# A two-block transformer kernel on one core: lat's weights in two transfers, ada0's column stage joined to ada1's, the memory input loaded and transposed earlier

## The reference

```
# first block
h = rms(x, mix_norm_g); p = h @ w_in            # columns: q, kv, k_rot | hyena (3 x 512)
a = mla(p...)                                   # 8 heads, latents normalised, rope
h = hyena(p..., rfft(filters(hy_w1, b1, freq, w2, b2, w3, b3, decay)))
x = x + concat(rms(a), rms(h)) @ w_out
x = x + mem_xattn(rms(x, cross_norm_g), rms(mem, mem_norm_g))   # K, V of 256 memory tokens
x = x + hier_moe(rms(x))                        # 4 groups x 8 experts, 2 taken per token
# second block
mod = silu(c) @ w_ada + b_ada                   # 6 x 1024 shifts, scales and gates
u = modulate(x, ...); x = ... hybrid_mixer(u)   # RG-LRU and block attention
u = modulate(x, ...); x = ... hierarchical_moe(u)
```

## Time and profile before

| | us |
|---|---|
| median of 3 runs | 1044.98 |
| lowest, highest | 1040.83, 1046.42 |
| the profiled execution | 1044.6 |
| its span (first to last instruction) | 1042.6 |
| PE busy in the span | 996.1 |
| DVE busy | 586.5 |
| ACT busy | 351.5 |
| POOL busy | 20.2 |

### The profile page before, as it was taken

How to read it: one execution, slowest core, us unless ns; L and a number is a source line. 1 busy time by engine, 2 the same in 40 slices (tenths; PEclk the granted TensorE clock), 3 DMA queues, 4 the chain that set the end, 5 groups by cost and what they waited for, 6 DMA issues and landing times.

```text
span 1042.6 us, 15038 instructions
## 1 busy us (share of the span) xinstructions
PE 996.1 (96%) x5360; PEld 606.1 (58%) x5360; DVE 586.5 (56%) x1105; ACT 351.5 (34%) x676; POOL 20.2 (2%) x41
## 2 busy tenths in 40 slices
PE   8999999999999999999999999999989999999985
PEld 7668566977968633434344579876753434434434
DVE  5735427555355646444444585787765655555546
ACT  5653424445444222212222355743531111111113
POOL 1000001000000000000000000000000000000000
PEclk9999999999998999999999999989999999999998
DMA  9255572446408499999999828430709999999931
GB/s 362 114 238 212 210 302 108 162 182 242 162 1 332 167 368 425 426 425 425 424 427 424 356 81 360 171 156 1 282 12 385 424 425 424 428 423 427 423 133 41
DMA packets 28896, 289.06 MB, mean 277 GB/s; under 512 B 3080, under 2 KB 5544, under 8 KB 7728
## 3 DMA queue, kind: packets, MB, share of 16 engines
q1 hardware_dynamic: 25344, 282.04, 66.0%
q0 software_dynamic: 1136, 3.74, 1.2%
q10 hardware_dynamic: 2368, 2.64, 0.8%
HBM read 287.34 MB, written 1.06 MB: 277 GB/s over the span
## 4 chain that ended last, share of the span: by engine, by line
PE 52%; DVE 9%; ACT 3%; issue 2%; DVEq 1%; ACTq 0%
PE bank L977 22%; PE bank L991 11%; PE bank L997 6%; PE bank L984 4%; PE bank L625 1%; DVE ring_r L482 1%; PE bank L627 1%; PE bank L626 1%; PE bank L1097 1%; PE bank L950 1%; PE bank L1098 1%; ACT ring_r L475 1%; PE bank L1086 0%; PE bank L1138 0%; PE bank L1052 0%
## 5 line engine op out<-in xcount | busy, mean ns | idle before, releaser
L977 PE MATMUL bank<-ring,arena 128*64 128x512 f32 x1040 | 237.5, 598 | 1.4 <-DVE arena L2218 1.4
L482 DVE TENSOR_TENSOR ring_r<-ring,ring_r 128x1024 fp32r<-128x1024 f32 (+1 forms) x84 | 99.2, 1212 | 91.3 <-ACT ring_r L475 91.3
L2232 DVE TENSOR_REDUCE arena<-bank 128x512 f32 x130 | 83.7, 686 | 118.7 <-PE bank L997 116.1
L977 PEld LDWEIGHTS bank<-ring,arena 128*64 128x64 f32 x1040 | 69.3, 136 | 123.8 <-issue 123.8
L991 PE MATMUL bank<-ring,arena 128*64 128x512 f32 x520 | 127.4, 611 | 1.8 <-DVE arena L2354 1.5
L475 ACT ACTIVATE ring_r<-ring 128x1024 fp32r<-128x1024 f32 (+1 forms) x84 | 84.8, 1046 | 83.2 <-PE bank L627 82.1
L625 PE MATMUL bank<-HT_r,ring_r 128*128 128x256 f32 x352 | 102.0, 290 | 7.1 <-DVE arena L1899 3.2
L627 PE MATMUL bank<-HT_r,ring_r 128*128 128x256 f32 x352 | 100.3, 285 | 0.0
L1568 ACT ACTIVATE arena<-bank 128x512 f32<-128x512 f32 x64 | 38.3, 598 | 150.9 <-PE bank L977 150.9
L997 PEld LDWEIGHTS bank<-tab,arena 128*128 128x128 f32 x520 | 55.7, 140 | 55.6 <-issue 49.6
L625 PEld LDWEIGHTS bank<-HT_r,ring_r 128*128 128x128 f32 x352 | 68.2, 194 | 10.4 <-issue 8.9
(11 more groups left out here) (429 smaller groups left out, 1422.5 us busy)
## 6 DMA issues: line engine op xcount, KB each, us to landing
ring<-in_experts SPq DMA_DIRECT2D x64, 2048.0 KB, 15.1
ring<-in_experts SPq DMA_DIRECT2D x64, 1024.0 KB, 11.5
ring<-in_ada SPq DMA_DIRECT2D x12, 2048.0 KB, 9.7
ring<-in_win SPq DMA_DIRECT2D x5, 2048.0 KB, 12.7
ring<-in_hy SPq DMA_DIRECT2D x3, 2048.0 KB, 19.1
ring<-in_mk SPq DMA_DIRECT2D x2, 2048.0 KB, 8.7
ring<-in_mv SPq DMA_DIRECT2D x2, 2048.0 KB, 9.6
ring<-in_wo SPq DMA_DIRECT2D x2, 2048.0 KB, 7.5
```

The source lines that it names most:

```text
L482: nc.vector.tensor_tensor(R(w), w, R(h), ALU.subtract).then_inc(sem("w_low"), 1)
L977: last = mm(gu_bank[g:g + WIN, :], xw[:, k, :], w[:, k * 512:(k + 1) * 512], start=k < 2, stop=k >= KD - 2)
L2232: last = V.reduce_sum(ysT[:, 4 * u:4 * u + 4, bass.ds(s, WIN)], dT_bank[u][:, :].rearrange("p (c g w) -> p c w g", c=4, g=2), AXX)
```

## The change

1. The first quarter of lat's weights becomes a transfer of its own with its own semaphore (`lat_in`), issued ahead of the filters' argument inputs (`feat`); the rest of lat is issued behind them. ACT and DVE split chunk 0 of lat before they evacuate hT(0, 1). On DVE the first sine argument is moved behind these evacuations. The filler ahead of lat has 3 pairs in place of 5.
2. ada0 is pinned to bank 6. Its column stage adac0 goes, and ada_col(1) does the columns of ada0 and ada1 together. ada0's slot is vacated with ada1's. All later banks of the rotation change.
3. The memory tokens get a buffer of their own in the arena, free after the first spectrum product. ACT issues their load at the first head, and squares them at the fourth and fifth; DVE normalises them at the sixth. PE transposes them ahead of the second convolution, the filler ahead of mk goes, and DVE takes their low parts before `gated(1)`.
4. Two pairs of semaphores in the router become two semaphores; DVE waits once where it waited twice.
5. The fillers ahead of cnt2 and gx2 have 10 pairs in place of 8. Three matmuls of 256 columns follow gu_T in the extra window.

```diff
-          ("hy1", 2), ("hyT0", 2), ("latT", 2), ("ada0", 1), ("hy2", 2), ("hyT1", 2), ("adac0", 1),
+          ("hy1", 2), ("hyT0", 2), ("latT", 2), ("ada0", 1, (6,)), ("hy2", 2), ("hyT1", 2),
...
-STAGES += [("cv1", 2), ("memT", 4), ("mk", 4), ("mv", 4), ...
+STAGES += [("memT", 4), ("cv1", 2), ("mk", 4), ("mv", 4), ...
...
 LAST.update({f"ada{_i}": (f"adac{_i}", 0) for _i in range(12)})
+LAST["ada0"] = LAST["ada1"]
...
-        junk, junk_m = area(16384, 1024), area(4096, 1024)
+        junk = area(16384, 1024)
+        mem, junk_m = three(area(4096, 2048), TT), hytok[:, :, 0, :]
...
-            arrived(act, name)
+            if (name, chunks) == ("lat", (0,)):
+                act.wait_ge(sem("lat_in"), 16)
+            else:
+                arrived(act, name)
...
+            sp.dma_start(ring[:, slot(1), 0:2 * LAT], A["lat"][:, 0:2 * LAT]).then_inc(sem("lat_in"), 16)
             sp.dma_start(ring[:, slot(0), at:at + FEAT], A["filt"][:, at:at + FEAT]).then_inc(sem("feat"), 16)
-            load(PLACE["lat"], A["lat"], dict(UNITS)["lat"])
+            sp.dma_start(ring[:, slot(1), 2 * LAT:KD * LAT], A["lat"][:, 2 * LAT:KD * LAT]
+                         ).then_inc(sem(f"slot_full{slot(1)}"), 16)
...
             def ada_col(i):
-                ready(pe, f"ada{i}")
+                parts = (0, 1) if i == 1 else (i,)
+                for n in parts:
+                    ready(pe, f"ada{n}")
                 ps = take(pe, f"adac{i}")
-                for c in range(4):
-                    last = mm(ps[:, c:c + 1], ada_sum(i)[:, c * P:(c + 1) * P], ones[:, 0:1], start=True, stop=True)
+                for a, n in enumerate(parts):
+                    for c in range(4):
+                        last = mm(ps[:, 4 * a + c:4 * a + c + 1], ada_sum(n)[:, c * P:(c + 1) * P], ones[:, 0:1],
+                                  start=True, stop=True)
...
-            occupy("lat", 0, 5, still[:, 0:P], still[:, P:P + 256])
+            occupy("lat", 0, 3, still[:, 0:P], still[:, P:P + 256])
...
             hyena_tok(1)
-            ada_col(0)
...
+            transposed("memT", mem, KD, "xn_m")
             convolve(1)
-            transposed("memT", XN, KD, "xn_m")
-            occupy("mk", 0, 5)
-            channel_out("mk", ["mk0", "mk1"], HT, low_m, banks_of("memT"))
+            channel_out("mk", ["mk0", "mk1"], HT, low_x, banks_of("memT"))
...
-                occupy(f"cnt{b}", 0, 8 if b == 2 else 6)
+                occupy(f"cnt{b}", 0, 10 if b == 2 else 6)
...
-                occupy(f"gx{b}", 0, 8 if b == 2 else 6)
+                occupy(f"gx{b}", 0, 10 if b == 2 else 6)
...
                         gu_T().then_inc(sem(f"extra_gT{b}"), 1)
+                        for _ in range(3):
+                            mm(d_bank[0][:, 0:256], ident, T("iota")[:, 0:256], start=True, stop=True)
...
+            high(act, "lat", (0,))
             high_evac("hT", HT, (0, 1), lambda k: C("mix_norm_g", k))
-            high(act, "lat", (0,))
+            high(act, "lat", (1,))
             high_evac("hT", HT, (2, 3), lambda k: C("mix_norm_g", k))
-            high(act, "lat", (1,))
...
-                if h + 2 == H1 - 1:
-                    act.dma_start(XN, A["mem"]...).then_inc(sem("mem_in"), 16)
+                if h == 0:
+                    act.wait_ge(sem("product"), TT)
+                    act.dma_start(mem, A["mem"]...).then_inc(sem("mem_in"), 16)
+                if h in (3, 4):
+                    act.wait_ge(sem("mem_in"), 16)
+                    act.wait_ge(sem("zed"), TT)
+                    square(junk_m, three(mem[:, h - 3, :], 2), ssq_m[:, h - 3:h - 2])
             high(act, "mk0", (0, 1))
-            act.wait_ge(sem("mem_in"), 16)
-            squares("m", lambda t: XN[:, t, :], lambda t: junk_m, ssq_m, lambda t: None)
...
-                act.wait_ge(sem("e_diff"), b)
-                A_(ex2, m2, ACT.Exp).then_inc(sem("e_exp"), 1)
-                act.wait_ge(sem("g_diff"), b)
-                A_(gex, cand4, ACT.Exp).then_inc(sem("g_exp"), 1)
+                act.wait_ge(sem("diffs"), 2 * b - 1)
+                A_(ex2, m2, ACT.Exp).then_inc(sem("exps"), 1)
+                act.wait_ge(sem("diffs"), 2 * b)
+                A_(gex, cand4, ACT.Exp).then_inc(sem("exps"), 1)
...
-            sine_argument("f1", "hy_b1", C("hy_freq", 0, 1, FFN))
+            low(dve, "lat", (0,))
             got(dve, "hT", 3)
             low_evac("hT", HT, low_x, (0, 1), lambda k: C("mix_norm_g", k))
-            low(dve, "lat", (0,))
+            sine_argument("f1", "hy_b1", C("hy_freq", 0, 1, FFN))
+            low(dve, "lat", (1,))
             low_evac("hT", HT, low_x, (2, 3), lambda k: C("mix_norm_g", k))
-            low(dve, "lat", (1, 2, 3))
+            low(dve, "lat", (2, 3))
...
-            modulation(0)
...
                 if h == 5:
+                    normalised("m", lambda t: mem[:, t, :], lambda t: mem[:, t, :], rstd_m, "xn_m")
                     spectrum_product(1)
-            normalised("m", lambda t: XN[:, t, :], lambda t: XN[:, t, :], rstd_m, "xn_m")
             low(dve, "mk0", (0, 1))
+            low_evac("memT", HT, low_x, 4, lambda k: C("mem_norm_g", k))
             gated(1)
             dve.wait_ge(sem("zed"), 2 * TT)
-            low_evac("memT", HT, low_m, 4, lambda k: C("mem_norm_g", k))
...
-                dve.wait_ge(sem("e_exp"), b)
-                dve.wait_ge(sem("g_exp"), b)
+                dve.wait_ge(sem("exps"), 2 * b)
```

More of the change, by code:

```diff
@@ L184 @@
         STAGES += [("zs1", 4)]
-STAGES += [("cv1", 2), ("memT", 4), ("mk", 4), ("mv", 4), ("mixT", 4), ("wo", 4), ("ada7", 1), ("cT", 4), ("adac7", 1), ("mq", 4),
+STAGES += [("memT", 4), ("cv1", 2), ("mk", 4), ("mv", 4), ("mixT", 4), ("wo", 4), ("ada7", 1), ("cT", 4), ("adac7", 1), ("mq", 4),
            ("xs0", 1), ("xs1", 1)]
@@ L853, in _ @@
                     z_spectrum(1)
+            transposed("memT", mem, KD, "xn_m")
             convolve(1)
-            transposed("memT", XN, KD, "xn_m")
-            occupy("mk", 0, 5)
-            channel_out("mk", ["mk0", "mk1"], HT, low_m, banks_of("memT"))
-            token_out("mv", ["mv0", "mv1"], HT, low_m, banks_of("memT"))
+            channel_out("mk", ["mk0", "mk1"], HT, low_x, banks_of("memT"))
+            token_out("mv", ["mv0", "mv1"], HT, low_x, banks_of("memT"))
             for j in range(4):
@@ L1427, in _ @@
                     mla_exp(h + 2)
-                if h + 2 == H1 - 1:
-                    act.dma_start(XN, A["mem"].rearrange("(t p) d -> p t d", p=P)).then_inc(sem("mem_in"), 16)
+                if h == 0:
+                    act.wait_ge(sem("product"), TT)
+                    act.dma_start(mem, A["mem"].rearrange("(t p) d -> p t d", p=P)).then_inc(sem("mem_in"), 16)
+                if h in (3, 4):
+                    act.wait_ge(sem("mem_in"), 16)
+                    act.wait_ge(sem("zed"), TT)
+                    square(junk_m, three(mem[:, h - 3, :], 2), ssq_m[:, h - 3:h - 2])
             high(act, "mk0", (0, 1))
-            act.wait_ge(sem("mem_in"), 16)
-            squares("m", lambda t: XN[:, t, :], lambda t: junk_m, ssq_m, lambda t: None)
             ready(act, "pv7")
@@ L1886, in modulation @@
                 ps = got(dve, f"adac{i}")
-                m = mod[:, 4 * i:4 * i + 4]
-                free(V.tensor_tensor(m, ps[:, 0:4], C("b_ada_2", 4 * i, 4), ALU.add), f"adac{i}")
+                i0 = 0 if i == 1 else i
+                n = 4 * (i + 1 - i0)
+                free(V.tensor_tensor(mod[:, 4 * i0:4 * i0 + n], ps[:, 0:n], C("b_ada_2", 4 * i0, n), ALU.add), f"adac{i}")
             def outer_taps(third):
@@ L2138, in moe @@
                 V.tensor_tensor(M12, M1, M2, ALU.add).then_inc(sem("hot"), 1)
-                V.tensor_tensor(m2, i2, m1, ALU.subtract).then_inc(sem("e_diff"), 1)
+                V.tensor_tensor(m2, i2, m1, ALU.subtract).then_inc(sem("diffs"), 1)
                 V.tensor_tensor(cand4, lgg, gmx.unsqueeze(2).broadcast_to([P, TT, G]), ALU.subtract
-                                ).then_inc(sem("g_diff"), 1)
+                                ).then_inc(sem("diffs"), 1)
                 if b == 1:
```

## The result

The changed kernel takes 1041.75 us (median of 12 runs, 1039.65 to 1044.11) against 1044.51 (12 runs, 1040.83 to 1048.4). The ratio is 0.9974, interval 0.9962 to 0.9986: 2.8 us faster, where 7 were forecast. The time lies in the forecast's range and the direction is right, but the gain is 2.8 of 7.0 us, within the 0.5% that I called no change. The profiled execution took 1040.8, its span 1038.3.

What follows compares the result with a forecast made beforehand. PE, busy for 96% of the span, was taken as the bound. The terms -1.7 - 4.6 + 0 + 4.7 - 3.1 - 0.7 - 1.6 = -7.0 took the median 1044.98 to 1038.0 us, range 1030.5 to 1045.0.

Steps and rivals of the forecast that it cites:

- The start: First lat projection: with its first quarter loaded early, PE starts sooner and the last layer comes earlier; gain 1.7 us.
- Rival (d): Start: the new order changes nothing, since the sine argument takes lat's place; 1039.7 us, chance 0.11.
- hy2's banks: At hy2: banks freed earlier remove 3.0 us of PE's wait and the 1.6 us slow stretch behind; gain 4.6.
- ada0's columns: ada column stages: eight small matmuls move to ada1's stage and cancel those removed; 0 us.
- ada3: Attention stage: late slot release delays ada3's load; 2.95 us stall plus 1.7 slow stretch, a loss of 4.7.
- the signs of being wrong: ada3 landing over 10 us after issue, mk waiting for DVE, or attention-stage clock falling for longer than 4 us.
- My step for the memory's share: ada3's load: the memory input beside it takes bandwidth and delays its landing by 1.3 us, bounds 0 and 2.5.
- The memory part: Memory stage: transposes ahead of the second convolution let mk follow it directly; gain 3.1 us.
- yl: Before the yl projection: the shifted bank rotation removes PE's 0.69 us wait for a copy; gain 0.7 us.
- The extra window: Extra window: three matmuls fill 1.45 us of idle, so the eight following take 1.96 instead of 3.51; gain 1.6.
- The router's fillers: Second router: the longer fillers add 0.9 us, each into a wait such as 1.65 us; 0 us.
- Rival (a): Attention stage and others: ada3's stall eats most of the gain, slow stretches stay; 1044 us, half 1041; chance 0.22.

Runs made afterwards that it cites:

- before; again: The unchanged kernel before, run once more for a second profile: 1042.9 us, one run.
- 1 slot early: The changed kernel with ada0's slot freed after its product: 1037.63 us, ratio 0.9938 to the kernel before.
- 2 own column: The changed kernel with ada0's own column stage on a pinned bank and its slot freed as in the kernel before: 1037.67 us, ratio 0.9932.
- 3 own column, late: The changed kernel with ada0's own column stage, its slot still released with ada1's: 1040.96 us, ratio 0.9977 to the kernel before.
- 4 short fill: The changed kernel with 8 pairs in place of 10 in the second router's two fillers: 1040.67 us, ratio 0.9965 to the kernel before.
- 5 argument first: The changed kernel with ada0's slot freed early and the filters' argument inputs issued ahead of lat's first quarter: 1038.65 us, ratio 0.9933.
- 6 old start: The changed kernel with ada0's slot freed early and the start part undone: 1037.53 us, ratio 0.9938 to the kernel before.
- 7 memory later: The changed kernel, slot still late, with the memory input issued at the third head and its squares one head later: 1039.43 us, ratio 0.9949.
- 8 no cover: The changed kernel with ada0's slot freed early, without the three matmuls in the extra window: 1038.44 us, ratio 0.9930.
- 10 old memory part: The changed kernel with ada0's slot freed early and the memory part as in the kernel before: 1041.3 us, ratio 0.9965.
- 11 banks only: The kernel before with only the bank and column part of the change, ada0's slot freed after its product: 1040.69 us, ratio 0.9956.
- 12 combined: The changed kernel with ada0's slot freed early, the old start and the second router's short fillers: 1038.39 us, ratio 0.9932.

## Why the prediction was wrong

Three quantities from the fourteen profiles, in us, each from the timeline of PE, carry the verdicts (L921 is the router's first line in the kernel before; it is L929 in the changed one):

| kernel | filters' last layer starts | hy2's first matmul to the last V product | second router's L921 to the first expert |
|---|---|---|---|
| before; again | 26.40; 25.24 | 84.33; 84.33 | 27.55; 27.57 |
| changed | 25.41 | 87.47 | 29.58 |
| 1 slot early | 25.39 | 82.97 | 27.53 |
| 2 own column | 27.19 | 82.98 | 27.95 |
| 3 own column, late | 26.53 | 90.11 | 27.50 |
| 4 short fill | 25.77 | 88.71 | 27.50 |
| 5 argument first | 27.93 | 82.98 | 29.64 |
| 6 old start | 26.37 | 82.98 | 29.62 |
| 7 memory later | 26.33 | 85.89 | 29.61 |
| 8 no cover | 26.21 | 82.97 | 27.53 |
| 10 old memory part | 27.00 | 84.62 | 29.60 |
| 11 banks only | 26.24 | 84.63 | 28.75 |
| 12 combined | 26.39 | 84.65 | 27.60 |

**The start (forecast -1.7): wrong, 0.** The eight kernels with the new start (5 set apart) have the last layer at 26.2 in the mean (25.4 to 27.2), the five with the old one at 26.1 (25.2 to 26.4). The step that failed is "filt's argument about 1.0 to 1.4 later". In all eight it lands at 9.6 to 10.0, 2.2 to 2.6 later than the 7.34 of the earlier trace rows. I left out the 0.47 us by which SP issues it later (3.05 for 2.58), and took the landing of a small transfer as its bytes over the rate. So in the changed kernel the argument (L683, now L690) moves by 2.5 us and the transposes behind it by 1.6 (8.76 to 10.37), not by the 0.2 to 0.5 of the forecast. PE then idles for 1.7 to 3.4 us, where it had under 0.6 in four of the five profiles of the old start. In six of the eight a slow stretch begins there and ends before 17 us; three of the five old starts have one too. The second stop, at lat's second chunk, came, 1.65 later than forecast (17.75 for 16.1), and that is what the last layer is late by (25.41 for 23.7). Kernel 11, with the old start, an argument landing at 9.9 and no slow stretch, has its last layer at 26.24, 1.0 later than the second profile of before; so a late argument costs the old start too. Rival (d) had the value right, no gain at the start, but not the reason.

**hy2's banks (-4.6): right.** 3.9 at hy2, less the 1.0 that came from the start in that profile, is 2.9 of wait. The slow stretch behind it went in every profile: 84.33 in the table against 82.97 makes 1.4, together 4.3. Kernel 11 has 4.6 by its ratio for this and yl, where 5.3 were forecast.

**ada0's columns (0): right**, kernels 1 and 2.

**ada3 (+4.7): right in its mechanisms, about right in its size.** The column of the table grows from 82.97 to 87.47, 88.71 and 90.11 with the late slot, by 4.5, 5.7 and 7.1, the last beyond my bound of 5.9, and by 2.9 with the memory input out of the way. The medians give 4.1 (changed less kernel 1) and 3.3 (kernel 3 less 2), the ratios 3.8 and 4.7. In the changed kernel's own profile a slow stretch ahead of ada3 took part of the time that PE would else have waited, so it is in part luck that its 4.5 meets 4.7: I had 2.95 of stall and 1.7 behind it, and it has 1.52 of stall and a slow stretch on either side. The sentence that an idle of 3 us was twice followed by a slow stretch misread its rows: one of the two idles was 2.06 us, and in the second profile of before 2.30 us at the same place had none. Of the signs of being wrong that I had named the changed kernel showed none: 9.1 us for ada3's landing, no wait of mk for DVE, two slow stretches of 3.4 us each. Kernel 3, with the same late slot, showed two: 10.8 us, and a slow stretch of 6.8.

My step for the memory's share (1.3, from the 12.2 us in the earlier trace rows) was too low: 1.7 to 3.4. I had set the Trainium skill's rule ("DMA: Bandwidth & Descriptors", Queues, rings and completion order: turns between queues) aside by that row. Where ACT issues the memory input 0.7 us ahead of the ada load, as in the changed kernel and in kernels 1, 4, 5, 6, 8 and 12, it lands in 4.9 to 5.4 us. 4.9 is 214 GB/s, half of the 426 that the window shows; that fits turns of equal size, and their 2.5 for ada3 is near the 1.7 to 2.2 measured there. But in kernels 2 and 3 it was issued 0.2 us behind the ada load and took 17.4 and 16.8, and in kernel 7, issued behind three of SP's loads that were still under way, 17.7. Equal turns alone don't give that, and why the order weighs so much stays open. The 12.2 of the row lies between: its memory input was issued behind a load that was still under way.

**The memory part (-3.1): right**, 3.6 in the profiles (12.74 to 9.16), and 3.7 between the medians of kernels 10 and 1 (2.8 by their ratios).

**yl (-0.7): right.** Before, 20.5 us after the wait at 638.46 came another of 0.69; it is gone in every profile with the new banks.

**The extra window (-1.6): half of it.** The forecast took one slow stretch for the rule. Without the three matmuls it came in two profiles of four (3.51 and 3.57 us for the eight matmuls, against 1.94 and 1.94), with them in none of ten. The mean gain is 0.8, from four profiles.

**The router's fillers (0): wrong, about +1.** The step "0.9 us, each into a wait such as the 1.65" holds only at full clock. In the nine profiles with long fillers the stage took 27.5 us where the clock held (three), 27.95 with a shorter slow stretch, and 29.6 in all five where it fell for 6 us or more. The two longer fillers can't be left early: at half clock the first ends after its data are there (6.81 us for 20 instructions in place of 16). With short fillers it took 27.5 to 27.6 four times and 28.75 once, with slow stretches in three of the five; the 28.75 is the only one of them with a slow stretch as long as 6.8 us, and 0.85 less than the 29.6. The stage by itself misleads, though, because a slow stretch in it goes with less time just before it (the last section). From L1207 (products at 682 us, ahead of the router) to the first expert all nine with long fillers took 90.5 to 90.9, the five with short ones 88.7, 89.1, 89.8, 90.1 and 90.7, which is 1.1 less in the mean. How much of this is the fillers' own and how much the chance of slow stretches is not shown. The medians (kernel 4 against the changed one, -1.1) agree and don't prove it.

The sum with these values, 0 - 4.3 + 4.5 - 3.6 - 0.7 - 0.8 + 1.0, is -3.9, against -2.8 measured with an interval of -1.5 to -4.0. With 5.8 for ada3, the mean of its three profiles, it would be -2.6; one profile of each kernel doesn't settle the sum closer. So two terms failed, the start (1.7) and the fillers (1.0), and that of the extra window was twice too large (0.8): 3.5 of the 4.2 us that were missing. All three had been taken from a single execution's slow stretches or waits, or from bytes over a rate. Rival (a) comes nearest to what was measured, in its milder form at 1041, but it put the loss mainly on ada3 and on hy2's slow stretch, which went. That the time lies in the range says little for the sum: the range reached over both rivals.

**Open.** The stretch at 118 to 121 came in four of ten profiles with the 16-matmul column stage (changed, 10, 11, 12) and in none of the four without it. Kernels 1 and 4 to 8 show that the stage doesn't bring it about every time; whether it makes it likelier isn't settled. It costs 1.65 where nothing hides it (82.98 to 84.63). Another one between 161 and 170 us, at the end of the heads, came in kernels 8, 10, 11 and 12 alone; in kernels 8 and 12 it costs 1.65 (10.8 us to mk in place of 9.16). Nor is it settled why the argument inputs land late.

## What to carry to other kernels

Before two resources are given back together, look at what the later release holds up: here one line of bookkeeping took back more than half of the gain, although the next tenant's bytes didn't touch what was still in use. A slow stretch of the clock in one profile is a term of the sum only if a second execution shows it too; the one behind hy2's wait of 3.2 us came in both profiles with the wait, that behind the extra window's 1.45 us in two of four. A filler in front of data that was sized at full clock may cost time when the clock falls. And a stage whose slow stretches move about is compared together with its neighbours, not alone.

## What the runs showed of the hardware

A small transfer's landing does not follow from its place in the queue. With the order argument inputs, lat's quarter, rest of lat, the 95.5 KB of `col` issued ahead of all of them took 8.0 us to land, in place of 3.9 in the changed kernel and 4.5 before; the argument inputs took 7.8, 6.7 and 4.7. In kernel 11, whose start is the old one, they landed at 9.9 all the same, in a profile with these rows:

```profile
ring<-in_filt SPq DMA_DIRECT2D x1, 192.0 KB, 7.3
...
col<-in_col SPq DMA_DIRECT2D x1, 95.5 KB, 7.4
```

The four other profiles of the old start, with the same transfers in the same order, have 4.4 to 4.7 and 3.9 to 4.7 there. So an execution can shift these landings by 3 us with nothing changed, and a single profile doesn't show what an order of transfers does. What the eight profiles of the new start do show is 6.5 to 6.9 for the argument inputs each time.

Between 680 and 745 us a slow stretch can be the cheaper course for a while. Where PE runs slow at 685 to 691, as in the changed kernel, its wait for DVE behind that is 1.0 us or less, and it comes from L1207 to the router in 61.3 us (682.04 to 743.35). Where it keeps its clock there, it waits 3.4 us for DVE, runs slow right after, and takes 63.2 (in kernel 1, 677.83 to 741.06). With the long fillers the router takes the 2 us back: the first course has a slow stretch in it (29.6 in the table), the second none (27.5), and both reach the experts in 90.7 to 90.9. In kernel 8 the wait is this row:

```profile
699.62 0.65 PE L1254 MATMUL bank<-arena 128*64 128x256 f32 x2 [3.44 <-DVE arena L2563]
```
